# First block's scan of states read from PSUM, and the steps beside both attentions dealt anew

## The chip, the cores and the metric

The kernel runs on one core of a Trainium2 chip. The time is the device time of one execution in microseconds (us). The engines named below are PE (TensorE, the matrix engine; PEld is its weight load), DVE (VectorE), ACT (ScalarE), POOL (GpSimd) and SP (SyncE, which issues the transfers). All data is float32. SBUF is the on-chip memory that every engine reads; PSUM is the memory that PE writes, here two tensors `acc` and `wrk` of four banks each, 128 partitions by 512 numbers a bank.

## The reference, cut to what matters

Two transformer blocks of two layers each run one after the other on 256 tokens of width 1024. Of a layer of the first block only the mixer matters here:

```python
mod = silu(c) @ w_ada[l] + b_ada[l]      # 6 x 1024: shifts, scales, gates; layer 0 needs them first
a_out = dsa_mixer(aq, ak, av, ...)       # 6 heads of attention, 256 tokens, top-64 mask
b_out = hgrn2_mixer(bq, bf, bi, bg, ...) # 6 heads of a gated recurrence
#   state = exp(b_last) * state + k^T v  # one 64 x 64 state a head, a decay for each row
x = x + g1 * (concat(a_out, b_out, c_out) @ w_out[l])
```

A layer of the second block has three kinds of heads, the projections that feed them, and a retention:

```python
o_nsa = nsa_mixer(...)          # 6 heads, 3 branches each: compressed, selected, window
o_mla = mla_mixer(...)          # 5 heads; q and k come from latents cq, ckv by small matmuls
o_ret = retention_mixer(...)    # 5 heads, needs rq, rk, rv, rg
x = x + concat(o_nsa, o_mla, o_ret) @ w_out[l]
```

## The kernel before, in words

The order of the instructions on each engine is written out by hand. Each engine runs its own list, and waits on counters (`pe_done`, `act_done`, `dve_done`, `pool_done`) that the others raise; nothing is reordered.

**An attention** (`att_pe`, `att_act`, `att_dve`) runs over units, a unit being one branch of one head. Units go in pairs. For a unit PE computes the scores (L1023, into `wrk` banks 0 and 1), DVE masks them and takes the maximum (L1085, L1089), ACT takes the exponential (L1138), DVE divides (L1102, L1106), PE turns the result (L1036), ACT copies it back to SBUF (L1153), and PE multiplies by the values (L1056, L1058). DVE then copies the head's sum from `acc` (L1130). This chain has waits in it, and a function `beside(u)` lays other work into it, at unit `u`, on each engine.

**The first block.** Six units. The recurrence works in 16 blocks of 16 tokens: a loop of 16 bands on PE and DVE (L1380, L1496 to L1522) computes what happens inside a block, and its last piece is named "band end". Then the keys are turned (L1389). For each of three pairs of heads, `kv_pe` (L1405) makes the key-value products of all 16 blocks into `acc` banks 2 and 3 (8 matmuls of 256 columns on quarter tiles of the array, 64 by 64, called a set below), `kv_act` (L1417) copies them to SBUF in another order, `states_dve` (L1555) runs the recurrence over the blocks with two scans in place, and `inter_pe` (L1434) multiplies by the queries. PE makes the sets beside units 0, 1, 2 and the `inter` products beside units 3, 4, 5; the scans stand beside units 2, 3, 4. A set may start only when ACT has copied the one before it.

In layer 0 four column groups of `w_ada` (6 to 9) stand between band end and the attention, as steps "a" and "s": "a" is 8 matmuls of 512 columns (L672), which ACT copies (L680), "s" is 4 matmuls of one column that sum the copy (L687), and DVE adds the bias (L695, `mods`). In the tables "a 6" and "s 6" are the two for group 6.

**The second block.** 23 units: 18 of the first kind of heads (12 with full scores, then 6 with 15 columns) and 5 of the second kind (units 18 to 22). The table `BESIDE` gives for each unit the steps beside it: "p" is a projection (8 matmuls, L877, L880 or L893, copied by ACT), "r" a rotary turn (one matmul L922 and three DVE instructions L931 to L936), "m" a small product of a latent (L3027, copied by ACT at L3048). The steps alternate between `acc` banks 2 and 3, so the PE part of step n waits until step n-2 has been read. Units 18 to 22 need all "m" steps and the rotary turns of the "mq" ones.

Of the kernel before, what the change touches and what calls it, by code (L numbers as in the profile page):

```python
# [9 lines left out]
ALU = mybir.AluOpType  # L10
# [4 lines left out]
S = 256  # L15
# [3 lines left out]
HD = 64  # L19
# [147 lines left out]
def stream_items():  # L167
# [27 lines left out]
    for layer in range(DEPTH):  # L195
        after += [("in2", layer, i) for i in range(3)] + [("cmp", layer)] + [("in2", layer, i) for i in range(3, 6)]
        after += [("mla", layer), ("in2", layer, 6), ("decay", layer)] + [("out2", layer, h) for h in range(2)]
# [41 lines left out]
def program(nc, given, out, known, stop=None, dumps=None):  # L239
# [3 lines left out]
    with ExitStack() as ctx:  # L243
# [765 lines left out]
        def head_sum(b):  # L1009

            return acc[b["p0"]:b["p0"] + HD, b["head"] % 2, b["col"]:b["col"] + S]
# [238 lines left out]
        def branches1(l):  # L1250
            out = []
            for h in range(6):
                p0, j = HD * (h % 2), h // 2
                out.append(dict(q=s_q[p0:p0 + HD, j, :], k=s_k[p0:p0 + HD, 0, :], v=lambda t: s_v[:, t, :], mask=s_mask, head=h,
                                kind="causal", scale=float(HD) ** -0.5, gate=None, opens=True, last=True, p0=p0, col=0,
# [93 lines left out]
        r_pick = [Z(o, 4, HD) for o in (5888, 6144, 6400, 4352, 10640, 10896, 11152, 1536, 12176, 12432, 12688, 12944)]  # L1349
# [42 lines left out]
        def kv_pe(pe, l, a):  # L1392
# [17 lines left out]
        def kv_act(act, l, a):  # L1410
            if a == 2:
                act.wait_ge(dve_done, at("dve", "c out", l, 1))

            act.wait_ge(pe_done, at("pe", "kv", l, a))
            by_half = r_state[a].rearrange("p v (t r b) -> p r t b v", t=2, r=2)
# [117 lines left out]
        def picks_pool(pool, l, a):  # L1533
# [6 lines left out]
            else:  # L1540
                pool.wait_ge(dve_done, at("dve", "band end", l) if l else at("dve", "mods", 0, 9))
# [6 lines left out]
        def states_dve(dve, l, a):  # L1548

            dve.wait_ge(act_done, at("act", "kv", l, a))  # L1550
            dve.wait_ge(pool_done, at("pool", "wide", l, a))
            wide = r_wide[a].rearrange("p v b -> p (v b)")
            for i in range(HD // SCAN):
                part = r_state[a][:, SCAN * i:SCAN * (i + 1), :].rearrange("p v b -> p (v b)")
                dve.tensor_tensor_scan(part, wide, part, 0.0, ALU.mult, ALU.add)\  # L1555
                   .then_inc(dve_done, up("dve", "states", l, a) if i == HD // SCAN - 1 else up("dve"))
# [257 lines left out]
        def act_from(wait_names):  # L1814
# [6 lines left out]
        BESIDE_BANDS[0].update({8: ("a 4", "a 5"), 9: ("s 4", "s 5"), 10: ("p bg1",), 12: ("p bg2",),  # L1821
                                15: ("a 6", "a 7", "s 6", "a 8", "s 7", "a 9", "s 8", "s 9")})
        BESIDE_BANDS[1].update({8: ("p bg1",), 10: ("p bg2",)})
# [1891 lines left out]
```

## Time and profile before

| | us |
|---|---|
| median of 3 runs | 2350.98 |
| lowest, highest run | 2350.53, 2360.26 |
| the profiled execution's own time | 2354.34 |
| its span, first to last instruction | 2352.2 |

| stage of the profiled execution | from, us | to, us |
|---|---|---|
| first block, layer 0: last band matmul to output projection | 150.67 | 194.21 |
| first block, layer 1: scores of the attention to output projection | 586.38 | 616.55 |
| second block, layer 0: from the turned unit 11 to the retention | 1651.40 | 1707.80 |
| second block, layer 1: the same | 2041.15 | 2097.80 |

In a row of the timeline the first two numbers are the start and the length. A bracket at its end gives how long the engine stood idle just before, and what released it. A matmul in float32 leaves two records, so "x16" is 8 matmuls. A row whose instructions had a gap between them is longer by the gap. PEclk is the clock that PE was granted, 1.00 being 2.4 GHz and 0.50 being 1.2 GHz.

### The profile page before, as it was taken

To read this page: it belongs to the slowest core of one execution; us is meant where nothing else is said; L and a number is where in the kernel's file an instruction comes from. 1 tells how busy PE (TensorE), PEld (TensorE's weight loads), DVE (VectorE), ACT (ScalarE), POOL (GpSimd) and SP (SyncE) were. 2 spreads that over 40 slices of the span, in tenths; PEclk is the share of its full clock that TensorE was granted. 3 is DMA by queue.
4 is the path that set the end of the run, shared out by engine and by line. 5 is a ranking of instruction groups with operands and counts; after the bars stand their busy time and mean duration, and the time that the engine had idled before them with its cause. 6 is when DMAs were issued, how large, how long until landed. Compare 5 with 4: busy or idle time off the path is not lost.

```text
span 2352.2 us, 36220 instructions
## 1 busy us (share of the span) xinstructions
PE 2264.7 (96%) x15501; PEld 1596.1 (68%) x15502; DVE 920.6 (39%) x2174; ACT 381.8 (16%) x893; POOL 27.6 (1%) x52
## 2 busy tenths in 40 slices
PE   7989999999999999998999999989999999999999
PEld 5868998877763434433444444357679998769999
DVE  3663887548420000000000000034657734547764
ACT  3231100022320000000000000025421002531100
POOL 1010000001000000000000000000000000000000
PEclk8997999999899999999999999999999999999999
DMA  9571478944069999999988999992325463423441
GB/s 349 187 251 37 157 255 299 378 143 143 14 240 374 373 412 410 408 411 409 407 299 355 409 410 409 413 325 92 107 72 179 164 188 117 159 74 108 167 157 54
DMA packets 242163, 582.98 MB, mean 248 GB/s; under 512 B 24250, under 2 KB 108738, under 8 KB 229716
## 3 DMA queue, kind: packets, MB, share of 16 engines
q1 hardware_dynamic: 241428, 580.52, 66.6%
q8 instruction: 125, 2.05, 0.4%
q14 instruction: 34, 0.28, 0.0%
q0 software_dynamic: 576, 0.13, 0.0%
HBM read 579.58 MB, written 1.05 MB: 247 GB/s over the span
## 4 chain that ended last, share of the span: by engine, by line
PE 87%; DMA 6%; DVE 4%; ACT 1%; SPq 1%; issue 1%; DVEq 0%; ACTq 0%
PE wrk L2496 13%; PE acc L877 9%; PE acc L3335 5%; PE acc L3303 5%; PE acc L2556 5%; PE wrk L2481 4%; PE wrk L3335 4%; PE wrk L3303 4%; DMA ring<-in_moe_w_gate_dram 3%; PE acc L880 3%; PE acc L1660 3%; PE wrk L2503 3%; PE acc L1680 3%; PE wrk L1660 3%; PE acc L954 2%; PE acc L2539 2%
## 5 line engine op out<-in xcount | busy, mean ns | idle before, releaser
L2496 PE MATMUL wrk<-ring,hT 128*64 128x512 f32 (+1 forms) x1792 | 348.7, 542 | 11.8 <-DMA ring<-in_moe_w_up_dram 5.8
L2740 DVE TENSOR_TENSOR scratch<-scratch,wrk 128x512 f32<-128x512 f32 (+4 forms) x32 | 24.5, 767 | 793.2 <-PE wrk L2496 584.5
L2496 PEld LDWEIGHTS wrk<-ring,hT 128*64 128x64 f32 x1792 | 125.7, 137 | 211.7 <-issue 186.3
L877 PE MATMUL acc<-hT,ring 128*128 128x256 f32 x1024 | 231.7, 381 | 3.7 <-DVE scratch L936 2.9
L877 PEld LDWEIGHTS acc<-hT,ring 128*128 128x128 f32 x1024 | 191.4, 190 | 33.7 <-DVE scratch L936 3.9
L2556 PE MATMUL acc<-ring,scratch 128*64 128x512 f32 x784 | 177.2, 597 | 8.5 <-DMA ring<-in_moe_w_down_dram 7.7
L3380 DVE TENSOR_TENSOR ring<-ring 128x512 f32<-128x512 f32 (+1 forms) x192 | 155.2, 863 | 1.2
L2556 PEld LDWEIGHTS acc<-ring,scratch 128*64 128x64 f32 x784 | 53.8, 136 | 113.1 <-issue 101.8
L3335 PE MATMUL acc<-scratch,ring 128*128 128x128 f32 x1024 | 117.6, 275 | 0.0
L3335 PEld LDWEIGHTS acc<-scratch,ring 128*128 128x128 f32 x1024 | 116.0, 192 | 0.0
L2675 ACT ACTIVATE scratch<-wrk 128x512 f32<-128x512 f32 (+4 forms) x32 | 21.1, 661 | 483.6 <-PE wrk L2528 483.6
L2481 PE MATMUL wrk<-ring,hT 128*128 128x512 f32 x224 | 96.9, 593 | 0.5 <-DMA ring<-in_moe_w_gate_dram 0.5
L3335 PE MATMUL wrk<-scratch,ring 128*128 128x128 f32 x768 | 89.0, 275 | 0.0
L3303 PE MATMUL acc<-mixT,ring 128*128 128x128 f32 x768 | 88.4, 275 | 0.0
L3335 PEld LDWEIGHTS wrk<-scratch,ring 128*128 128x128 f32 x768 | 87.4, 192 | 0.0
L3303 PEld LDWEIGHTS acc<-mixT,ring 128*128 128x128 f32 x768 | 87.0, 192 | 0.0
L880 PE MATMUL acc<-ring,hT 128*128 128x384 f32 (+5 forms) x384 | 81.3, 368 | 4.7 <-ACT scratch L910 2.9
L1680 PE MATMUL acc<-scratch,ring 128*128 128x256 f32 x352 | 77.2, 380 | 4.4 <-DMA ring<-in_ffn_w_down_dram 4.4
L910 ACT ACTIVATE scratch<-acc 128x256 f32<-128x256 f32 (+6 forms) x118 | 41.3, 361 | 231.9 <-PE acc L877 158.2
L2481 PEld LDWEIGHTS wrk<-ring,hT 128*128 128x128 f32 x224 | 42.3, 190 | 53.1 <-issue 53.1
L2503 PE MATMUL wrk<-ring,hT 128*32 128x256 f32 (+1 forms) x1536 | 77.6, 354 | 0.0
L880 PEld LDWEIGHTS acc<-ring,hT 128*128 128x128 f32 x384 | 60.7, 195 | 23.8 <-ACT scratch L910 4.3
(464 smaller groups left out, 3001.1 us busy)
## 6 DMA issues: line engine op xcount, KB each, us to landing
ring<-in_moe_w_gate_dram SPq DMA_DIRECT2D x56, 2048.0 KB, 19.1
ring<-in_moe_w_up_dram SPq DMA_DIRECT2D x56, 2048.0 KB, 21.1
ring<-in_moe_w_down_dram SPq DMA_DIRECT2D x56, 2048.0 KB, 22.6
ring<-in_w_ada_dram SPq DMA_DIRECT2D x24, 2048.0 KB, 17.0
ring<-in_w_up_dram SPq DMA_DIRECT2D x32, 1024.0 KB, 6.8
ring<-in_w_down_dram SPq DMA_DIRECT2D x32, 1024.0 KB, 6.4
ring<-in_w_out_dram SPq DMA_DIRECT2D x8, 2048.0 KB, 8.6
ring<-in_w_in_dram SPq DMA_DIRECT2D x10, 1536.0 KB, 9.6
```

What stands on the lines that cost most here:

```text
L877: mm = pe.matmul(acc[p0:p0 + m, bank, 0:S], cols(k), hT[:, k, :], start=(k == 0), stop=(k == KD - 1))
L880: mm = pe.matmul(acc[:, bank, 0:m], hT[:, k, t], cols(k), start=(k == 0), stop=(k == KD - 1))
L954: pe.matmul(accv[:, 4 * h + m, :], w[:, k, m * P:(m + 1) * P], mixT[:, k, :], start=(k == ks[0] and m % 2 == 0), stop=False, skip_group_ch ...
L1660: mm = pe.matmul(PRODUCT[x][:, t * P:(t + 1) * P], stationary[x][:, k, t * P:(t + 1) * P], moving[x][:, k, :], start=(k == 0), stop=(k == ...
L1680: mm = pe.matmul(accv[:, m, :], w[:, j, m * P:(m + 1) * P], DENSE_TILES[:, 4 * g + j, :], start=(g == 0 and j == 0 and m % 2 == 0), stop=( ...
L2481: mm = pe.matmul(flat_wrk[:, lo + c * 512:lo + (c + 1) * 512], hT[:, k, 0:P], w[:, at_, c * 512:(c + 1) * 512], start=(k == 0), stop=(k == ...
L2496: mm = pe.matmul(flat_wrk[h * HD:h * HD + HD, lo:lo + n2], hT[:, k, 0:HD], w[:, at_, h * n2:(h + 1) * n2], start=(k == 0), stop=(k == KD - ...
L2503: mm = pe.matmul(flat_wrk[quarter(c), lo + n2:lo + n2 + n4], hT[:, k, LIGHT:MIDDLE], w[:, at_, c * n4:(c + 1) * n4], start=(k == 0 and n2 ...
L2556: mm = pe.matmul(acc[h * HD:h * HD + HD, 0, :], turned[:, at_:at_ + HD], w[:, j, h * 512:(h + 1) * 512], start=(g == 0 and n == 0), stop=( ...
L3303: mm = pe.matmul(up_region(x)[:, t * P:(t + 1) * P], stationary[x][:, k, t * P:(t + 1) * P], moving[x][:, k, :], start=(k == 0), stop=(k = ...
L3335: mm = pe.matmul(PRODUCT[x][:, m * P:(m + 1) * P], stationary[x][:, t, m, :], moving[x][:, t, :], start=(i == 0 and t == 0 and m == 0), st ...
L3380: ins = dve.tensor_tensor(part(out_), part(a), part(b), ALU.subtract)
```

## The change

Four things change.

**The scan reads PSUM.** `kv_pe` now makes the products in the order in which the scan reads them: 16 matmuls of 128 columns (32 values by 4 blocks), each written with a stride of 16 numbers in its bank, in two turns, the second of which waits until the first has ended (PE waits on its own counter). The moving operand is read with its two inner dimensions swapped. `kv_act` is gone. `states_dve` scans straight from `acc` banks 2 and 3 into SBUF, beside units 0, 1 and 2 instead of 2, 3 and 4. A set waits for the two scans of the one before; the first `inter` waits for the scans of the third set.

**The a and s steps of layer 0** leave the place ahead of the attention and stand beside its units (`BESIDE_UNITS`), all in `acc` bank 0. Both heads of a pair now use bank 1. "a 7" waits until DVE has read "s 6", and so on.

**The second block's steps** from unit 12 on are dealt anew: the "m" steps go forward and stand in groups of three, the projections rv0, rv1, rg1, rg2 go back to units 18 to 21, and one rotary turn stands beside each unit. The loads of `w_in_2` part 5 and of the latents' weights swap places.

**Small ones.** Four of POOL's buffers (`r_pick` 8 to 11) move, since their old place is now in use, and with it goes POOL's wait for the s steps; `gain_dve(0, 1)` stands behind the attention.

```diff
         def kv_pe(pe, l, a):
...
-                pe.wait_ge(act_done, at("act", "kv", l, a - 1))
+                pe.wait_ge(dve_done, at("dve", "states", l, a - 1, 1))
             pe.wait_ge(pool_done, at("pool", "pick", l, 4 * a + 3))
-            for t in range(2):
-                for turn in range(2):
-                    for h in range(2):
-                        r = HD * ((h + turn) % 2)
-                        mm = pe.matmul(acc[HD * h:HD * h + HD, 2 + r // HD, S * t:S * t + S], r_kT[r:r + HD, 2 * a + t, HD * h:HD * h + HD],
-                                       r_pick[4 * a + 2 * h + t][r:r + HD].rearrange("p b v -> p (b v)"), start=True, stop=True,
-                                       skip_group_check=True)
-            mm.then_inc(pe_done, up("pe", "kv", l, a))
-
-        def kv_act(act, l, a):
...
-            for r in range(2):
-                act.activation(by_half[:, r], acc[:, 2 + r, :].rearrange("p (t b v) -> p t b v", t=2, v=HD), ACT.Copy)\
-                   .then_inc(act_done, up("act", "kv", l, a) if r else up("act"))
+            for turn in range(2):
+                if turn:
+                    pe.wait_ge(pe_done, at("pe", "kv half", l, a))
+                for t in range(2):
+                    for r in range(2):
+                        i = (r + turn) % 2
+                        own = acc[:, 2 + i, :].rearrange("p (v t r b) -> p t r v b", t=2, r=2, b=4)
+                        rows = slice(HD * r, HD * r + HD)
+                        for h in range(2):
+                            mm = pe.matmul(own[HD * h:HD * h + HD, t, r], r_kT[rows, 2 * a + t, HD * h:HD * h + HD],
+                                           r_pick[4 * a + 2 * h + t][rows, :, SCAN * i:SCAN * (i + 1)].rearrange("p b v -> p v b"),
+                                           start=True, stop=True, skip_group_check=True)
+                mm.then_inc(pe_done, up("pe", "kv" if turn else "kv half", l, a))
...
         def inter_pe(pe, l, a):
-            pe.wait_ge(dve_done, at("dve", "states", l, a))
+            pe.wait_ge(dve_done, at("dve", "states", l, a, 1))
             if a == 0:
-                pe.wait_ge(act_done, at("act", "kv", l, 2))
+                pe.wait_ge(dve_done, at("dve", "states", l, 2, 1))
...
         def states_dve(dve, l, a):
 
-            dve.wait_ge(act_done, at("act", "kv", l, a))
             dve.wait_ge(pool_done, at("pool", "wide", l, a))
+            dve.wait_ge(pe_done, at("pe", "kv", l, a))
...
-                dve.tensor_tensor_scan(part, wide, part, 0.0, ALU.mult, ALU.add)\
+                dve.tensor_tensor_scan(part, wide, acc[:, 2 + i, :], 0.0, ALU.mult, ALU.add)\
...
+        BESIDE_UNITS = ((("a 6",), ("s 6", "a 7"), ("s 7", "a 8"), ("s 8", "a 9"), ("s 9",), ()), ((),) * 6)
+        MODULATED = sum(BESIDE_UNITS[0], ())
...
+        def step1_bank(l, n):
+
+            return 0 if steps1(l)[n] in MODULATED else bank1(n)
...
+            def beside(u):
+                if u < 3:
+                    states_dve(dve, l, u)
+                for step in BESIDE_UNITS[l][u]:
+                    step1_dve(dve, l, step)
+                if u == 5:
+                    head_sum_dve(dve, l)
...
-                  ("p rq2", "r kpe"), ("p rk1", "r rq0"), ("p rk2", "m mq0"), ("p rk0", "m mq1", "r mq0"),
+                  ("p rq2", "r kpe"), ("p rk1", "r rq0"), ("m mq0", "m mq1", "m mk0", "r rq1"), ("p rk2", "r mq0"),
```

On PE, in layer 0 of the first block, these rows stood one after the other (L672 an a step, L687 an s step, L1389 the turned keys, L1405 a set, L1023 scores, L1036 a turned unit):

```order
L672 MATMUL acc<-ring,vec_rows 32x512 x16
L687 MATMUL acc<-const,scratch 128x1 x4
L672 MATMUL acc<-ring,vec_rows 32x512 x8
L687 MATMUL acc<-const,scratch 128x1 x4
L672 MATMUL acc<-ring,vec_rows 32x512 x8
L687 MATMUL acc<-const,scratch 128x1 x8
L1389 MATMUL acc<-const,mixT 128x128 x6
```

and in the changed kernel, from the turned keys on (L1410 is the new set):

```order
L1410 MATMUL acc<-scratch 64x32x4 x16
L687 MATMUL acc<-const,scratch 128x1 x4
L672 MATMUL acc<-ring,vec_rows 32x512 x8
L1036 MATMUL wrk<-const,scratch 128x128 x3
L1410 MATMUL acc<-scratch 64x32x4 x16
L687 MATMUL acc<-const,scratch 128x1 x4
L672 MATMUL acc<-ring,vec_rows 32x512 x8
```

The keys and the scores now come first, and each a step stands behind a set and an s step, ahead of the next turned unit.

On DVE the changed kernel has at the same place, behind the masks and the division of a unit, the two scans and the bias of the s step (L695), ahead of the next unit's mask:

```order
L1106 TENSOR_SCALAR scratch<-scratch,stat 128x128
L1106 TENSOR_SCALAR scratch<-scratch,stat 128x256
L1548 SCALAR_TENSOR_TENSOR hT<-scratch,acc 128x512 x2
L695 TENSOR_TENSOR mods<-acc,vec 128x4
L1085 ISA scratch,stat<-wrk,scratch 128x128
```

So "a 7", which waits for L695, waits for both scans too.

On PE in the second block, at units 12 to 14, the difference is this (L3027 before and L3031 after are the m steps, L893 and L877 projections, L922 a rotary turn, L1033 a turned unit, L1023 scores):

```order
-L893 MATMUL acc<-hT,ring 64x256 x16
-L3027 MATMUL acc<-scratch,ring 96x256 x2
+L877 MATMUL acc<-hT,ring 128x256 x8
 L922 MATMUL acc<-scratch,const 96x256
 L1033 MATMUL wrk<-const,scratch 15x128 x2
-L3027 MATMUL acc<-scratch,ring 96x256 x2
-L3027 MATMUL acc<-scratch,ring 64x256
+L3031 MATMUL acc<-scratch,ring 96x256 x2
+L3031 MATMUL acc<-scratch,ring 64x256 x2
```

A projection is followed by one rotary turn, and the m steps have moved together.

## Rows read from the trace of the kernel before

**Rows 1.** The page: PE's share of the span, and the chain by engine.
```profile
PE 2264.7 (96%) x15501; PEld 1596.1 (68%) x15502; DVE 920.6 (39%) x2174; ACT 381.8 (16%) x893; POOL 27.6 (1%) x52
...
PE 87%; DMA 6%; DVE 4%; ACT 1%; SPq 1%; issue 1%; DVEq 0%; ACTq 0%
```

**Rows 2.** Timeline of PE, first block, layer 0.
```profile
151.22 3.64 PE L672 MATMUL acc<-ring,vec_rows 128*32 128x512 f32 x32
154.79 1.05 PE L687 MATMUL acc<-const,scratch 128*128 128x1 f32 x8
...
162.27 0.85 PE L1389 MATMUL acc<-const,mixT 128*128 128x128 f32 x6
...
164.03 1.09 PE L1405 MATMUL acc<-scratch 64*64 64x256 f32 x16
165.94 0.93 PE L1023 MATMUL wrk<-scratch 64*128 64x128 f32 x8 [0.82 <-DVE stat L1089]
...
169.00 1.09 PE L1405 MATMUL acc<-scratch 64*64 64x256 f32 x16 [1.33 <-ACT hT L1417]
...
172.12 1.99 PE L1405 MATMUL acc<-scratch 64*64 64x256 f32 x16 [1.55 <-ACT hT L1417]
...
194.21 3.78 PE L954 MATMUL acc<-mixT,ring 128*128 128x256 f32 x8
...
208.81 4.58 PE L954 MATMUL acc<-mixT,ring 128*128 128x256 f32 x20
```

**Rows 3.** Timelines of DVE and ACT, same place: band end, scans, copy.
```profile
153.07 0.69 DVE L1522 TENSOR_TENSOR mixT<-mixT,scratch 128x48 f32<-128x48 f32 x1
...
170.83 2.33 DVE L1555 TENSOR_TENSOR_SCAN hT<-scratch,hT 128x512 f32<-128x512 f32 x2
...
167.06 1.89 ACT L1417 ACTIVATE hT<-acc 128x512 f32<-128x512 f32 x2
```

**Rows 4.** Stretches at half clock: window, length, busy by engine, PEclk, DMA, GB/s.
```profile
171.50:178.20 6.70, 6.08 (x41) 3.27 (x41) 4.01 (x13) 3.80 (x9) 0.00 (x0) 0.50 0.00 0
182.00:204.80 22.80, 21.99 (x173) 18.24 (x174) 7.05 (x15) 4.54 (x10) 0.00 (x0) 0.50 0.00 1
616.55:618.30 1.75, 1.75 (x6) 1.48 (x5) 1.54 (x3) 0.30 (x1) 0.00 (x0) 0.50 0.00 0
1707.40:1714.30 6.90, 6.50 (x28) 4.67 (x30) 2.35 (x6) 0.44 (x1) 0.00 (x0) 0.51 0.00 0
```

**Rows 5.** Timeline of PE, first block, layer 1: sets and first inter.
```profile
593.25 1.78 PE L1405 MATMUL acc<-scratch 64*64 64x256 f32 x16 [0.23 <-ACT hT L1417]
...
597.08 1.09 PE L1405 MATMUL acc<-scratch 64*64 64x256 f32 x16 [1.56 <-ACT hT L1417]
...
600.36 3.48 PE L1434 MATMUL acc<-scratch,hT 64*64 64x16 f32 x60
```

**Rows 6.** Groups by line and form, 160 to 195 us: quarter-tile weight loads.
```profile
L1434 PEld LDWEIGHTS acc<-scratch 64*64 64x64 f32 x60 | 3.4, 199 | 0.3 <-DVE mixT L1130 0.3
...
L1405 PEld LDWEIGHTS acc<-scratch 64*64 64x64 f32 x48 | 1.8, 160 | 4.4 <-ACT hT L1417 3.4 <-ACT scratch L1468 0.4 <-issue 0.4
```

**Rows 7.** Timeline of PE, second block, layer 1.
```profile
2041.15 3.62 PE L877 MATMUL acc<-hT,ring 128*128 128x256 f32 x16
...
2075.53 3.72 PE L877 MATMUL acc<-hT,ring 128*128 128x256 f32 x16 [0.32 <-DVE scratch L936]
...
2085.29 3.72 PE L877 MATMUL acc<-hT,ring 128*128 128x256 f32 x16 [1.13 <-DVE scratch L936]
...
2096.12 0.65 PE L1056 MATMUL acc<-scratch 128*64 128x256 f32 x2 [1.43 <-DVE mixT L1130]
...
2097.80 1.23 PE L3117 MATMUL wrk<-scratch 64*128 64x256 f32 x4 [0.60 <-DVE mixT L1130]
```

**Rows 8.** Timelines of DVE and ACT, same stage: latents, rotary turn, exponential.
```profile
2041.27 0.48 DVE L2960 SCALAR_TENSOR_TENSOR scratch<-scratch,vec 128x256 f32<-128x256 f32 x1
...
2042.77 0.42 DVE L936 TENSOR_TENSOR scratch<-scratch 64x256 f32<-64x256 f32 x1
...
2043.73 0.31 ACT L1138 ACTIVATE scratch<-scratch,stat 128x15 f32<-128x15 f32 x1 [0.87 <-DVE stat L1089]
```

More of the change, by code:

```diff
@@ L195, in stream_items @@
     for layer in range(DEPTH):
-        after += [("in2", layer, i) for i in range(3)] + [("cmp", layer)] + [("in2", layer, i) for i in range(3, 6)]
-        after += [("mla", layer), ("in2", layer, 6), ("decay", layer)] + [("out2", layer, h) for h in range(2)]
+        after += [("in2", layer, i) for i in range(3)] + [("cmp", layer)] + [("in2", layer, i) for i in range(3, 5)]
+        after += [("mla", layer), ("in2", layer, 5), ("in2", layer, 6), ("decay", layer)] + [("out2", layer, h) for h in range(2)]
         n = D_FF // 512
@@ L1009, in head_sum @@
         def head_sum(b):
-            return acc[b["p0"]:b["p0"] + HD, b["head"] % 2, b["col"]:b["col"] + S]
+            return acc[b["p0"]:b["p0"] + HD, b["bank"], b["col"]:b["col"] + S]
         def att_scores_pe(pe, tag, pair, branches):
@@ L1254, in branches1 @@
                 out.append(dict(q=s_q[p0:p0 + HD, j, :], k=s_k[p0:p0 + HD, 0, :], v=lambda t: s_v[:, t, :], mask=s_mask, head=h,
-                                kind="causal", scale=float(HD) ** -0.5, gate=None, opens=True, last=True, p0=p0, col=0,
+                                kind="causal", scale=float(HD) ** -0.5, gate=None, opens=True, last=True, p0=p0, bank=1, col=0,
                                 over=[h - 2] if h >= 2 else [], place=mixT[p0:p0 + HD, j, :],
@@ L1348, in program @@
         r_kT, r_squares = Z(7568, 6, P), Z(1536, 3, S)
-        r_pick = [Z(o, 4, HD) for o in (5888, 6144, 6400, 4352, 10640, 10896, 11152, 1536, 12176, 12432, 12688, 12944)]
+        r_pick = [Z(o, 4, HD) for o in (5888, 6144, 6400, 4352, 10640, 10896, 11152, 1536, 1792, 2048, 7184, 4608)]
         r_root = stat[:, 112:124]
@@ L1539, in picks_pool @@
                 pool.wait_ge(dve_done, at("dve", "band end", l))
-            else:
-                pool.wait_ge(dve_done, at("dve", "band end", l) if l else at("dve", "mods", 0, 9))
             for n in range(4 * a, 4 * a + 4):
@@ L1833, in steps1 @@
                 steps += BESIDE_BANDS[l].get(j, ())
-            return steps
+            return steps + sum(BESIDE_UNITS[l], ())
         def number1(l, name):
@@ L1841, in bank1 @@
             return n % 4 if n < FIRST_BESIDE else 2 + n % 2
+        def step1_bank(l, n):
+            return 0 if steps1(l)[n] in MODULATED else bank1(n)
         def bank1_read(l, n, bank):
-            users = [i for i in range(n) if bank1(i) == bank]
+            users = [i for i in range(n) if step1_bank(l, i) == bank]
             return step1_read(l, users[-1]) if users else None
@@ L1870, in step1_pe @@
             kind, _, name = step.partition(" ")
-            bank, bank_read = bank1(n), bank1_read(l, n, bank1(n))
+            bank, bank_read = step1_bank(l, n), bank1_read(l, n, step1_bank(l, n))
+            if step == MODULATED[0]:
+                bank_read = (act_done, at("act", "kT", l))
             if kind == "p":
@@ L1945, in beside @@
                     inter_pe(pe, l, u - 3)
+                for step in BESIDE_UNITS[l][u]:
+                    step1_pe(pe, l, step)
             att_pe(pe, tag, branches1(l), beside)
@@ L1990, in beside @@
             def beside(u):
-                if u < 3:
-                    kv_act(act, l, u)
+                for step in BESIDE_UNITS[l][u]:
+                    step1_act(act, l, step)
             att_act(act, tag, branches1(l), beside)
@@ L2036, in block1_dve @@
                     topk_mask_dve(dve, l)
+            def beside(u):
+                if u < 3:
+                    states_dve(dve, l, u)
+                for step in BESIDE_UNITS[l][u]:
+                    step1_dve(dve, l, step)
+                if u == 5:
+                    head_sum_dve(dve, l)
+            att_dve(dve, tag, branches1(l), beside)
             if l == 0:
                 gain_dve(dve, 0, 1)
-            def beside(u):
-                if 2 <= u < 5:
-                    states_dve(dve, l, u - 2)
-                elif u == 5:
-                    head_sum_dve(dve, l)
-            att_dve(dve, tag, branches1(l), beside)
             head_norm_dve(dve, l)
@@ L3078, in branches2 @@
                                 scale=float(HD) ** -0.5, gate=lambda t, c=3 * h + br: n_gate[:, t, c:c + 1], opens=br == 1 and i < 2,
-                                last=br == 0, head=2 * i + g_, p0=HD * (h % 2), col=S * (i // 2), over=[],
+                                last=br == 0, head=2 * i + g_, p0=HD * (h % 2), bank=g_, col=S * (i // 2), over=[],
                                 place=mixT[HD * (h % 2):HD * (h % 2) + HD, h // 2, :],
@@ L3088, in branches2 @@
                                 mask=K("causal"), kind="causal", scale=96.0 ** -0.5, gate=None, opens=True, last=True, p0=p0, head=6 + h,
-                                col=0, over=((0, 4), (1, 5), (6,), (7,), (8,))[h],
+                                bank=h % 2, col=0, over=((0, 4), (1, 5), (6,), (7,), (8,))[h],
                                 place=mixT[p0:p0 + HD, 3 + h // 2, :], mask_ready=[],
```

13 lines of the change are left out of this document (4 added, 9 removed), and 6 rows, old and new, of the table BESIDE.

## The prediction

> **What bounds the kernel now.** I read the page first: PE is busy for 96% of the span, and 87% of the chain that ended last runs through it [rows 1]. So only what PE does, or waits for, can move the time, and the evictions on ACT that the change removes are worth just the PE idle time they cause. Next I read the timeline of PE around the places that the diff touches, four stages of 30 to 60 us each. In the first block, layer 0, PE runs from 151.22 to 194.21, and from 151.22 to 162.27 it works through the a and s steps without a gap [rows 2]. The idle time comes behind: 1.33 and 1.55 us before the second and third set, both for ACT's copy, and 0.82 us before scores [rows 2]. The reader is to see that the a and s steps are not waits that can be filled but 11 us of PE work that only moves. In layer 1 the same two waits are 0.23 and 1.56 us [rows 5]. In the second block the idle time stands late, where two rotary turns share a unit: 0.32 and 1.13 us, and 1.43 and 0.60 us in the tail [rows 7]. Last I read the windows for the granted clock: PE runs at 1.2 GHz from 171.5 to 178.2 and from 182.0 to 204.8, in the tail of the second block for 6.9 us, but for only 1.75 us of layer 1's output projection [rows 4]. It fell after stretches with waits in them, and it rose after dense ones.
>
> All waits that the change can remove add up to some 12 us over the four stages, about 0.5% of the time, and about 0.5% is also what a measurement of this kernel can tell from no change.
>
> **One set.** Before, 8 matmuls of 256 columns take 1.09 us at full clock [rows 2]. Now there are 16 of 128 columns with the same number of columns in all, and PE waits once for its own first half. No row shows this form. The lower bound is 1.0 us, since the columns are the same (a gain of 0.1 has no mechanism here but is not excluded). The upper bound is what the columns take if the four quarter tiles don't overlap: the output projection takes 4.58 us for 20 records of 256 columns [rows 2], 0.23 us a record, so 0.23 us for two records of 128, and 16 times that is 3.7 us. The nearest row is `inter`, the other stream of quarter tiles: 30 matmuls in 3.48 us [rows 5], 0.116 us each, bound by how fast they follow each other. 16 of them take 1.9 us, and I take 2.0 with the wait in the middle. That is 0.9 us more a set at full clock; at half clock a set took 1.78 [rows 5] to 1.99 us already [rows 2], and there I add 0.2 us.
>
> The order of access is in doubt too. `inter` loads weights with a stride between its numbers and a load takes 199 ns; the load of a set, whose numbers lie side by side, takes 160 ns, although half of those ran at half clock [rows 6]. So a stride costs something on the read side. The Trainium skill, "SBUF — State Buffer" (section "Door 1: The DMA port swizzle"), says it in general: "any non-contiguous PSUM access pattern significantly slows down matmuls", and a read from SBUF is slowed once each access goes to another line of 16 bytes. By that rule a set nears 3.7 us and the sum is +9.7; by the row the stride costs a quarter of a load and the sum is the one below.
>
> **One scan pair** takes 2.33 us from SBUF [rows 3], 1.17 us for 512 numbers. Reading PSUM could cost more or nothing; DVE's masks and head copies read PSUM all along, and I keep 2.33, with 2.0 and 4.7 as ends (a small gain, or twice the time).
>
> **First block, layer 0.** Against 151.22 to 194.21:
> - three sets, 0.9 us each: +2.7;
> - the waits for ACT's copy go: 1.33 + 1.55 = -2.9; the 0.82 us before the scores is now covered by "a 6": -0.8;
> - the third set and the work to 178.2 ran at half clock. The set alone lost 1.99 - 1.09 = 0.9, and of 6.08 us busy [rows 4] at most half, 3.0, was lost. With four a steps in it this stretch should stay at full clock: -2.7;
> - at the start the scores need band end, 153.07 + 0.69 = 153.76 [rows 3], and the turned keys alone, 0.85 us, end at 152.1. The a steps used to cover this: +1.7;
> - "a 7" waits until DVE has added the bias of "s 6", and that stands behind the two scans, which wait for the set. From the end of the set DVE needs 2.33 and some 0.3 for the bias and hand-overs; PE has only the s step, 1.05 us [rows 2]. So PE idles 1.6 us, and again before "a 8"; before "a 9" the scans are done and about 0.3 is left: +3.5. Behind the waiting a step stands the turned unit on PE, for which ACT and the value matmuls wait.
> Sum: 2.7 - 2.9 - 0.8 - 2.7 + 1.7 + 3.5 = +1.5 us.
>
> The output projection behind it starts at 194.21 and stays at half clock until 204.8, 10.6 us, a loss of 5.3. In layer 1 the same stage is at half clock for 1.75 us, a loss of 0.9 [rows 4]. Where in this stage the clock rises is not set by the change, so I take the mean of the two, 3.1: -2.2 us.
>
> DMA and POOL are no term: the picks of the third set are ready before it, and the ring slots that the a steps free later hold weights of the next stage, some 40 us away.
>
> **First block, layer 1.** No a steps cover anything. Two sets at half clock and one at full: 0.2 + 0.2 + 0.9 = 1.3. A set waits for 2.33 of scans instead of 1.89 of copies [rows 3], +0.4 twice, less a part covered: +0.7. The first `inter`, which began at 600.36 without a wait [rows 5], now waits for the third set's scans: +0.4. Sum +2.4 us.
>
> **Second block,** for each layer. Spreading the rotary turns takes away 0.32 and 1.13, and with projections beside the last units half of the 1.43 goes: -2.1. The m steps come one projection earlier, and stop there: "m mq0" would start at 2041.15 [rows 7] but the latents are ready at 2041.75, and "m mq1" needs the bank of the rotary turn that ends at 2043.2 [rows 8]: +0.6 and +0.5. The third of the group waits for ACT, whose exponentials start at 2043.73 ahead of the copies [rows 8]; this and the other groups I set at +0.5, against 0.6 of smaller waits that go. Sum -1.1, in two layers -2.2 us.
>
> **Sum.** +1.5 - 2.2 + 2.4 - 2.2 = -0.5 us. The profiled execution took 2354.3 (span 2352.2 and 2.1 around it), so it would take 2353.8; it was 3.4 us above the median, which is in the scatter of the three runs. From the median 2351.0 I forecast 2350.5.
>
> **Rivals.**
> - *Strides* (slower). If the quarter tiles stop overlapping, a set takes 3.7 us, 1.7 above my value, six times: +10.2, so 2360.7. For it: the strided weight loads. Against it: 4 numbers still lie side by side in PSUM, and the strided loads of `inter` cost 39 ns, not a multiple. It decides the sign from about 2.1 us a set. A scan pair of 4.7 us would do as much, 2.4 at the five waits for scans, with nothing in the trace for it. Chance 0.15 together.
> - *Cheap sets* (faster). A set stays at 1.1 us: 0.9 off in each of four sets at full clock and 0.2 in two: 2346.5. Chance 0.17.
> - *Clock* (faster). Denser work keeps PE at 2.4 GHz: the rest of the output projection's loss (3.1), some 2.1 between 182 and 194, where `inter` does not scale with the clock, and half of 6.5 us busy in both tails (6.4): -12.1, so 2338.9. Against it: `inter` runs of 3.5 us stand in the same place, and the clock fell behind them before. In full 0.05, half of it (2344.7) 0.13.
> - *Waits win* (slower). The scans' waits let the clock fall in layer 0 as before (+2.7) and the groups of m steps eat the second block's gain (+2.2): 2355.4. Chance 0.2.
> - The forecast itself: 0.3, with 2348 to 2353 as its own range.
>
> Only the ends of the strides and the clock rivals reach 11.8 us, 0.5%. Faster 0.06, same 0.89, slower 0.05. The range 2342 to 2359 leaves out the full clock rival and the far end of strides.
>
> **What would show it.** Right: L1410 about 2.0 us a set; in layer 0 two idle stretches of about 1.6 us on PE before L672, released by DVE L695; in layer 1 the first L1429 some 2.4 us later after the first scores; in the second block no wait above 1 us before a projection from unit 17 on, and a new wait before L3031 at unit 12. The forecast is wrong if the sets are off by over 0.5 us, if the clock differs from before by more than 5 us of half clock in all, or if a stage that the diff does not touch changes its length.

## The result and the profile after

| | before | changed |
|---|---|---|
| median, us (12 runs each, side by side) | 2352.9 | 2362.45 |
| lowest, highest | 2348.32, 2360.42 | 2358.04, 2366.21 |
| profiled execution, its span | 2354.34, 2352.2 | 2358.04, 2356.1 |

The ratio is 1.0034, with a 95% interval from 1.0023 to 1.0044: by it the change makes the kernel about 8 us slower (the medians lie 9.5 us apart). All ratios here are of the fast executions; one of 5892 us and one of 2397 us, in the two kernels with moved code below, are left out. The forecast was 2350.5, within 2342 to 2359, and the measured median lies above that range. The profiled execution of the changed kernel was the fastest of its twelve, so the profiles differ by only 3.7 us. The stages below are therefore read in several profiles each.

The page of the changed kernel answers to [rows 1]: PE has 96 more matmul records (48 matmuls) and 96 more weight loads, and its share of the chain falls from 87 to 86%.

```profile
PE 2263.3 (96%) x15597; PEld 1594.1 (68%) x15598; DVE 920.9 (39%) x2174; ACT 371.4 (16%) x881; POOL 27.6 (1%) x52
...
PE 86%; DMA 6%; DVE 5%; issue 1%; SPq 1%; ACT 1%; DVEq 0%; ACTq 0%
```

The timeline of PE in layer 0 of the first block, changed kernel, answers to [rows 2]. L1410 is the new set.

```profile
149.57 0.62 PE L1380 MATMUL wrk<-scratch,const 128*128 128x24 f32 x4 [1.09 <-DVE scratch L1499]
...
152.81 1.40 PE L1023 MATMUL wrk<-scratch 64*128 64x128 f32 x8 [1.91 <-DVE mixT L1517]
154.14 2.58 PE L1410 MATMUL acc<-scratch 64*64 64x128 f32 x32
...
159.83 2.45 PE L1410 MATMUL acc<-scratch 64*64 64x128 f32 x32
...
164.96 1.92 PE L672 MATMUL acc<-ring,vec_rows 128*32 128x512 f32 x16 [1.70 <-DVE mods L695]
...
167.29 2.42 PE L1410 MATMUL acc<-scratch 64*64 64x128 f32 x32
...
172.38 2.50 PE L672 MATMUL acc<-ring,vec_rows 128*32 128x512 f32 x16 [1.69 <-DVE mods L695]
...
183.58 3.64 PE L672 MATMUL acc<-ring,vec_rows 128*32 128x512 f32 x16 [0.35 <-DVE mods L695]
...
201.76 3.24 PE L954 MATMUL acc<-mixT,ring 128*128 128x256 f32 x8
```

The waits are where the prediction put them: 1.91 us for band end, then 1.70, 1.69 and 0.35 us for the bias. The sets at full clock take 2.42 to 2.45 us instead of 1.09. "a 8" and "a 9" take 2.50 and 3.64 us where "a 7" takes 1.92: the clock is down again. On DVE the reason for the 1.70 us is plain, the scans (L1548) stand ahead of the bias, and they take the same 2.33 us from PSUM as from SBUF [rows 3]:

```profile
162.43 2.33 DVE L1548 TENSOR_TENSOR_SCAN hT<-scratch,acc 128x512 f32<-128x512 f32 x2 [1.27 <-PE acc L1410]
164.68 0.14 DVE L695 TENSOR_TENSOR mods<-acc,vec 128x4 f32<-128x4 f32 x1
```

Layer 1 of the first block (with [rows 5]) has its waits before the second and third set and, new, a short one before the first `inter` (L1429):

```profile
598.98 2.53 PE L1410 MATMUL acc<-scratch 64*64 64x128 f32 x32 [1.21 <-DVE hT L1548]
...
604.02 2.50 PE L1410 MATMUL acc<-scratch 64*64 64x128 f32 x32 [1.68 <-DVE hT L1548]
...
609.13 3.48 PE L1429 MATMUL acc<-scratch,hT 64*64 64x16 f32 x60 [0.18 <-DVE scratch L1548]
```

Then a place that the diff doesn't touch, the norm behind the experts of the first block (L837). PE stops in it for 2.43 us, released by nothing that the profile shows:

```profile
1565.98 0.51 PE L837 MATMUL wrk<-scratch,const 128*128 128x256 f32 x1
1568.92 0.48 PE L837 MATMUL wrk<-scratch,const 128*128 128x256 f32 x1 [2.43 <-issue]
```

In the kernel before this norm has no gap. And the tail of the second block, with [rows 7] and the last of [rows 4]: the retention's matmuls take 0.71 us instead of 1.23, at full clock, and 5.24 us pass from the first of them to the output projection, instead of 7.76.

```profile
2102.91 0.65 PE L1056 MATMUL acc<-scratch 128*64 128x256 f32 x2 [0.58 <-ACT scratch L1153]
...
2104.37 0.71 PE L3121 MATMUL wrk<-scratch 64*128 64x256 f32 x4 [0.60 <-DVE mixT L1130]
...
2109.61 4.58 PE L954 MATMUL acc<-mixT,ring 128*128 128x256 f32 x20
```

### The profile page after: what moved, and what is told of

It reads as the page before. It is cut to its first block, busy times and chain, and to the rows that moved or that the text cites. A ratio compares the mean times of both kernels' runs of the same rounds, so it can differ in the third digit from the quotient of the medians.

```text
span 2356.1 us, 36398 instructions
## 1 busy us (share of the span) xinstructions
PE 2263.3 (96%) x15597; PEld 1594.1 (68%) x15598; DVE 920.9 (39%) x2174; ACT 371.4 (16%) x881; POOL 27.6 (1%) x52
## 4 chain that ended last, share of the span: by engine, by line
PE 86%; DMA 6%; DVE 5%; issue 1%; SPq 1%; ACT 1%; DVEq 0%; ACTq 0%
PE wrk L2500 13%; PE acc L877 8%; PE acc L3339 5%; PE acc L3307 5%; PE acc L2560 5%; PE wrk L2485 4%; PE wrk L3339 4%; PE wrk L3307 4%; DMA ring<-in_moe_w_gate_dram 4%; PE acc L880 3%; PE wrk L2507 3%; PE acc L1653 3%; PE acc L1673 3%; PE wrk L1653 3%; PE acc L954 2%; PE acc L2543 2%
## 5 line engine op out<-in xcount | busy, mean ns | idle before, releaser
L877 PE MATMUL acc<-hT,ring 128*128 128x256 f32 x1024 | 231.4, 380 | 0.8 <-DVE hT L852 0.4
L877 PEld LDWEIGHTS acc<-hT,ring 128*128 128x128 f32 x1024 | 191.4, 190 | 29.8 <-issue 3.5
```

The costliest lines, as they stand in the source:

```text
L877: mm = pe.matmul(acc[p0:p0 + m, bank, 0:S], cols(k), hT[:, k, :], start=(k == 0), stop=(k == KD - 1))
```

## Parts alone

Four kernels take the change apart. "Scan" is the PSUM scan with its sets, "dealing" the a and s steps beside the units of layer 0, "table" the second block's steps and stream order.

The table alone (kernel before, with these lines of the change and the rest of the table, which the front shows in part):

```diff
-                  ("p rq2", "r kpe"), ("p rk1", "r rq0"), ("p rk2", "m mq0"), ("p rk0", "m mq1", "r mq0"),
+                  ("p rq2", "r kpe"), ("p rk1", "r rq0"), ("m mq0", "m mq1", "m mk0", "r rq1"), ("p rk2", "r mq0"),
```

> The kernel before with one part of the change: the second block's steps dealt anew (its table of steps and the stream's order). Theory A (the parts add up as the two profiles show them, the clock included): the two attentions of the second block are 0.5 and 0.9 us shorter in work and 2.6 and 2.5 us shorter in their retention tails, which run at the full clock; 6.5 us less in all, ratio 0.9972. Theory B (the tails' clock was the chance of one execution, only the work is shorter): 1.4 us less, ratio 0.9994, and the tail from the last projection's matmuls to the first output projection matmul of 20 keeps about 7.8 us in this profile. Between them: 3 to 4 us less if one tail in two runs at the full clock.

Measured: 0.9962 (0.9948 to 0.9975), 9 us faster. Theory A. Both tails run at full clock, as two windows of this kernel show, one over the whole attention of layer 0 and one over the last 64 us of layer 1's (window, length, PE busy and its records, PEclk, DMA, GB/s):

```profile
1591.88:1713.19 121.31, 115.97 (x734) 0.99 0.30 100
2036.00:2099.65 63.65, 58.48 (x324) 1.00 0.26 86
```

This is no chance. In all nine profiles of kernels with the new table both tails take 5.23 or 5.24 us; in the five with the old one they take 7.1 to 8.6. From the first waiting scores of the second block to layer 1's output projection the nine take 506.2 to 507.9 us and the five 512.8 to 518.5.

The first block alone (scan and dealing, old table; the edits from here on are against the changed kernel, and cut):

```diff
-                  ("p rq2", "r kpe"), ("p rk1", "r rq0"), ("m mq0", "m mq1", "m mk0", "r rq1"), ("p rk2", "r mq0"),
+                  ("p rq2", "r kpe"), ("p rk1", "r rq0"), ("p rk2", "m mq0"), ("p rk0", "m mq1", "r mq0"),
```

> The change without its second part: the first block changed (scan out of PSUM, adaptive steps dealt to the attention's units), the second block as before. Theory A: 9.5 us measured for the whole change plus the 6.5 us that the second block gives back, 16 us more, ratio 1.0068. Theory B: 9.5 plus 1.4, 11 us more, ratio 1.0046. The profile is to show the stretch from the end of the last band to the output projection of layer 0 at about 51 us against 43.0, and layer 1's at about 33.6 against 30.2 in either case.

Measured: 1.0073 (1.0059 to 1.0087), 17 us slower, theory A. With the table's -9 that makes the +8 of the whole: the two parts add.

The scan alone (with the old table too):

```diff
+                                15: ("a 6", "a 7", "s 6", "a 8", "s 7", "a 9", "s 8", "s 9")})
...
-        BESIDE_UNITS = ((("a 6",), ("s 6", "a 7"), ("s 7", "a 8"), ("s 8", "a 9"), ("s 9",), ()), ((),) * 6)
+        BESIDE_UNITS = (((),) * 6, ((),) * 6)
```

> The kernel before with the PSUM scan alone: products laid in the scan's order in two halves, no eviction, scans one unit apart; the adaptive steps stay behind the last band. Theory A (the dearer sets decide): each of the six sets is about 2.5 us instead of 1.1 to 2.0, and the units wait 1.2 to 1.7 us for the scan of the set before in layer 1; 3.4 us more in each layer, 7 us in all, ratio 1.0029. Theory C (the dealing of the adaptive steps is what costs, the scan is paid by the eviction it saves): 0 to 2 us more, ratio under 1.001.

Measured: 1.0039 (1.0025 to 1.0053), 9 us slower. That is theory A, whose 1.0029 lies within the interval, but not layer by layer: layer 0 is only 2.0 us longer and layer 1 4.3, where it has 3.4 for each. The rest is the stretch with the stop in the norm, 2.33 us here too, which the theory doesn't have.

The dealing alone (old table, and the old sets, copies and scans):

```diff
+                if u < 3:
+                    kv_act(act, l, u)
...
-                if u < 3:
-                    states_dve(dve, l, u)
+                if 2 <= u < 5:
+                    states_dve(dve, l, u - 2)
```

> The kernel before with the adaptive steps a 6 to s 9 dealt to the attention's units alone; key-value sets, evictions on ScalarE and scans as before. Theory A (waits of a 7 and a 8 came from VectorE's scans standing ahead of the reads in units 1 and 2; here the scans start at unit 2): the wait of a 7 goes, a 8 and a 9 keep one each, layer 0 gains the start of the attention but loses up to 5 us of clock in it; 0 to 3 us more, ratio 1.000 to 1.0013. Theory C (the dealing costs by itself, because TensorE runs thinner behind the last band and drops its clock): 6 us more or over, ratio 1.0026 or more, and the half clock covers more than 20 us of this stretch.

Measured: 1.0016 (1.0006 to 1.0025), 3.7 us slower, between the theories; layer 0 is 1.7 us longer, and no wait before an a step exceeds 0.35 us.

The stages, each from the timelines of the profiles (us):

| | layer 0: last band matmul to output projection | layer 1: scores to output projection | norm behind the experts to second block |
|---|---|---|---|
| before; table alone; before, code moved (below) | 43.5, 43.5, 43.5 | 30.2, 30.2, 30.1 | 36.0, 36.0, 41.0 |
| scan alone | 45.5 | 34.4 | 40.0 |
| dealing alone | 45.2 | 33.2 | 37.3 |
| changed; first block alone; changed, code moved | 52.2, 53.5, 53.0 | 33.6, 33.6, 33.7 | 40.1, 39.9, 37.2 |

So in layer 0 scan and dealing cost 2.0 and 1.7 us apart and 9.4 together. Only together do a set, two scans and an s step with its bias chase one another within one unit.

The table shows one thing more. With the dealing alone layer 1 is 3.0 us longer too, though its sets, copies and scans there are the old ones; of its edits only the bank of the heads' sums and the place of POOL's buffers, with its wait, reach that layer. Windows over the stage, first the kernel before, then the dealing alone:

```profile
586.38:616.55 30.17, 26.95 (x295) 0.67 0.01 4
```

```profile
582.34:615.56 33.22, 29.32 (x294) 0.55 0.01 4
```

Idle time grew by 0.7 us only (the wait before the second set is 1.33 instead of 0.23 us, the one before the third 1.19 instead of 1.56); the other 2.4 us are the same matmuls at a lower granted clock, 0.55 against 0.67. So 2 to 3 us of this stage can be clock alone, and what a kernel costs in it is not the price of its sets.

## The stop in a place that was not touched

All seven profiles of kernels with the long sets whose code is otherwise in its place show the stop (2.2 to 2.8 us), the three with the short ones don't. The sets added 192 instructions to PE's list, ahead of a jump: the experts' work is written twice, for few and for many tokens, and PE jumps over the second, which never runs here, straight to the norm. Two kernels move only what lies in that second part.

```diff
                 if k % 2:
                     mm.then_inc(last_share, 1)
+            for _ in range(126):
+                pe.wait_ge(last_weights, 1)
```

> The changed kernel with 64 more instructions in TensorE's code for the many-token case of the experts, which is jumped over in every run: nothing more is executed, only the code that the jump lands on moves by 64 places. The six longer sets added 192 instructions ahead of that jump, 192 plus 64 is 256. Theory F (the 2.2 to 2.4 us without a releaser in the norm behind the experts, seen in all three kernels with the long sets and in none without, is code that has not arrived behind the jump; it also keeps TensorE at half clock): the stall goes, the stretch from the first L837 to the first waiting L1023 of block two is 36 us again instead of 40.1, and the kernel is 4 us faster than the changed one: ratio to before 1.0017 instead of 1.0034. Theory N (the stall comes of the different times at which work arrives, not of where the code lies): no change, 1.0034.

> The kernel before with 192 instructions in the same code that is never run, so that the jump lands where it lands in the changed kernel. Theory F: a stall of 2.3 us in L837 after its seventh matmul and 4 us more in all, ratio 1.0017. Theory N: the same time as before, 1.0000, no stall.

The second has 382 waits in the same loop. Two waits make one instruction, so the loops make 63 and 191 instructions, one fewer than the expectations say. Measured: the changed kernel with the first loop 1.0021 (1.0006 to 1.0035), no stop, 37.2 us for the stretch instead of 40.1; the kernel before with the second 1.0016 (1.0004 to 1.0029), and 41.0 us instead of 36.0, with this in its timeline:

```profile
1556.54 0.63 PE L837 MATMUL wrk<-scratch,const 128*128 128x256 f32 x1
1559.99 0.80 PE L837 MATMUL wrk<-scratch,const 128*128 128x256 f32 x1 [2.83 <-issue]
```

It is the same matmul at which the changed kernel stops. So the place of the code decides it, as theory F has it: nothing more ran, and the kernel before got the stall and the changed one lost it. The two mended kernels below, with the first loop, are without the stop as well. In times the second is shown by its interval; the first agrees with -3 us but its interval touches the changed kernel's. The Trainium skill, "Runtime: NRT & Kernel Launch" (section "Instruction fetch mechanics"), says that instructions come in blocks of 256 and that a jump out of the window of two blocks forces a fetch. 192 + 63 = 255 fits but for one place: this move gave back nearly the old alignment. That a fetch is what PE waits for, and that the next block, just behind the landing place, is what comes late, is my reading of it; no run shows a fetch.

## What a set costs

> The changed kernel with its sets read and written in contiguous order (128 columns in a row out, four pieces of 32 in), so the scan's states are in another order than they should be; nothing else differs, and all sizes and counts stay. Theory L (a set is bound by its 32 matmuls with their weight loads and the wait for its own half, not by strides): a set still takes 2.3 to 2.6 us. Theory S (strides cost): a set falls to 1.7 us or less, half the columns' time and the wait of 0.55.

```diff
-                        own = acc[:, 2 + i, :].rearrange("p (v t r b) -> p t r v b", t=2, r=2, b=4)
+                        own = acc[:, 2 + i, :].rearrange("p (t r b v) -> p t r b v", t=2, r=2, b=4)
...
-                                           r_pick[4 * a + 2 * h + t][rows, :, SCAN * i:SCAN * (i + 1)].rearrange("p b v -> p v b"),
+                                           r_pick[4 * a + 2 * h + t][rows, :, SCAN * i:SCAN * (i + 1)],
```

Measured: 1.42 us a set at full clock, theory S; 2357.96 in its one run. Which side, reads or writes? One kernel makes only the writes contiguous, the other only the reads:

```diff
-                        own = acc[:, 2 + i, :].rearrange("p (v t r b) -> p t r v b", t=2, r=2, b=4)
+                        own = acc[:, 2 + i, :].rearrange("p (t r v b) -> p t r v b", t=2, r=2, b=4)
```

> The changed kernel with only the writes of its sets made contiguous (128 numbers in a row of PSUM in place of runs of four, 64 bytes apart); the pieces land in another order than the scans take them, so the states are of the wrong order. The reads stay strided (each number 256 bytes from the one before). With both made contiguous a set fell from 2.45 to 1.42 us. Theory R (the strided read of the moving operand costs it): a set at full clock stays at 2.4 us. Theory P (the strided write into PSUM costs it): it falls to 1.4 us. Both in part: about 1.9.

```diff
-                                           r_pick[4 * a + 2 * h + t][rows, :, SCAN * i:SCAN * (i + 1)].rearrange("p b v -> p v b"),
+                                           r_pick[4 * a + 2 * h + t][rows, SCAN * i:SCAN * (i + 1), :],
...
-                pool.tensor_tensor(r_pick[n], K("blocks4").unsqueeze(2).broadcast_to([P, 4, HD]),
-                                   b_i[:, t, (2 * a + h) * HD:(2 * a + h + 1) * HD].unsqueeze(1).broadcast_to([P, 4, HD]),
+                pool.tensor_tensor(r_pick[n], K("blocks4").unsqueeze(1).broadcast_to([P, HD, 4]),
+                                   b_i[:, t, (2 * a + h) * HD:(2 * a + h + 1) * HD].unsqueeze(2).broadcast_to([P, HD, 4]),
```

> The changed kernel, its result unchanged, with GpSimd laying down the masked products in the order in which the sets read them (value index outside, block inside), so that each matmul reads 128 numbers in a row; the writes into PSUM stay strided. Theory R: a set at full clock is 1.4 us, layer 0 loses 3 to 4 us of its 9.3, the waits of layer 1 for the scans take the place there; 3 to 4 us faster than the changed kernel, ratio to before 1.0018 to 1.0022. Theory P: sets stay at 2.4 us, ratio 1.0034. A danger for both: GpSimd's products may take longer in this order and come too late.

With contiguous writes alone, in one run of 2364.54 us, a set at full clock is as slow as ever:

```profile
162.38 2.44 PE L1410 MATMUL acc<-scratch 64*64 64x128 f32 x32
```

With contiguous reads, writes strided:

```profile
160.36 1.42 PE L1410 MATMUL acc<-scratch 64*64 64x128 f32 x32 [0.30 <-DVE hT L1548]
...
168.23 1.42 PE L1410 MATMUL acc<-scratch 64*64 64x128 f32 x32
...
594.61 2.35 PE L1410 MATMUL acc<-scratch 64*64 64x128 f32 x32 [1.66 <-DVE hT L1548]
```

The strided read costs 1.0 us a set, the strided write nothing. At half clock the set takes 2.35 us against 2.50 to 2.76, so the read costs only 0.2 to 0.4 there. Time: 1.0019 (1.0006 to 1.0031), 3.5 us less than the changed kernel. The two intervals overlap, so it is layer 0 that shows the gain, 49.3 us against 52.2 to 53.5. In layer 1 nothing came of it, 34.4 us against 33.6: its sets ran almost wholly at half clock (PEclk of the stage is 0.60 against 0.65), and the waits before the second and third grew from 2.9 to 3.35 us. POOL's products took 669 instead of 648 ns. What is left above the old 1.09 us is 0.3. The wait in the middle of a set, for which the weight loads idle 2.6 us over six sets, 0.4 each, would cover it; no run takes that wait away.

## Waits of the dealt steps, and mended versions

```diff
             def beside(u):
+                for step in BESIDE_UNITS[l][u]:
+                    step1_dve(dve, l, step)
                 if u < 3:
                     states_dve(dve, l, u)
-                for step in BESIDE_UNITS[l][u]:
-                    step1_dve(dve, l, step)
```

> The changed kernel with VectorE's order in the first three units turned: the read of the adaptive sums (L695) goes ahead of the scans. Theory A (the dealt steps wait because their bank's reader stands behind two scans): the waits of 1.70 and 1.69 us before L672 in units 1 and 2 shrink to under 0.7, and with less idle time less half clock: 3 to 6 us faster than the changed kernel, ratio to before 1.0008 to 1.0021. Theory W (the wait moves: now a scan waits for TensorE's sum and the next set waits for the scan): the waits before L1410 grow by as much, ratio 1.0034 as the changed kernel.

Measured: 1.0021 (1.0009 to 1.0033), 3 us less than the changed kernel. The intervals overlap here too, but both waits before L672 are 0.35 us, and layer 0 takes 48.6 us instead of 52.2 to 53.5, as theory A says; in layer 1 a set still waits 1.6 and 2.0 us for the scans.

```profile
165.82 3.55 PE L672 MATMUL acc<-ring,vec_rows 128*32 128x512 f32 x16 [0.35 <-DVE mods L695]
...
173.53 1.92 PE L672 MATMUL acc<-ring,vec_rows 128*32 128x512 f32 x16 [0.35 <-DVE mods L695]
```

The last two join the repairs: the scan alone with the new table, contiguous reads and moved code; and the whole change with all three. Of the first, beside the reads shown above:

```diff
-        BESIDE_UNITS = ((("a 6",), ("s 6", "a 7"), ("s 7", "a 8"), ("s 8", "a 9"), ("s 9",), ()), ((),) * 6)
+        BESIDE_UNITS = (((),) * 6, ((),) * 6)
...
+            for _ in range(126):
+                pe.wait_ge(last_weights, 1)
```

> The second block as changed, the PSUM scan with contiguous reads of its products, the adaptive steps left behind the last band, and the code behind the jump moved to where it lay before. By the terms measured so far, against the kernel before: layer 0 of the first block +2.0 less up to 3 for three cheaper sets, layer 1 +3.5 less up to 2, the code stall 0, the second block -8.5: -8 us in all, ratio 0.9966 (0.9953 to 0.998). It beats the second block's change alone (0.9962) only if the evictions that went on ScalarE had cost something that is not yet seen (rival: under 0.995).

> The changed kernel with all three repairs: contiguous reads in the sets, VectorE's reads of the adaptive sums ahead of the scans, code behind the jump moved by 64. By the single terms, if they add: 8.0 (changed kernel) less 4.3 (sums first), 3.9 (sets) and 4 (stall) is -4 us, ratio 0.9983. Rival (the repairs overlap, since all of them thin out the same waits and half-clock time): 0 us, ratio 1.000.

Measured: 0.9982 (0.9971 to 0.9992) and 0.9989 (0.9979 to 0.9998). Both beat the kernel before; neither beats the table alone, 0.9962. The second came out as its single terms add up. The first missed its expectation by 4 us: as the sets got cheaper the waits for the scans grew, in layer 0 to 1.69 and 2.00 us from 1.39 and 1.71, and layers 0 and 1 take 44.9 and 34.6 us, hardly other than the 45.5 and 34.4 of the scan alone.

```profile
168.59 1.42 PE L1410 MATMUL acc<-scratch 64*64 64x128 f32 x32 [1.69 <-DVE hT L1548]
...
172.54 2.35 PE L1410 MATMUL acc<-scratch 64*64 64x128 f32 x32 [2.00 <-DVE hT L1548]
```

So with the scans in PSUM the pace is theirs: both banks are taken until DVE has scanned, behind its own masks, while the old ACT copy freed them in 1.89 us and let the scans follow later. The best version measured is the kernel before with the second block's table alone.

## Why the prediction was wrong, step by step

| step | predicted | in the profiles (means of the rows named) |
|---|---|---|
| first block, layer 0 | +1.5 | +9.4 (52.9 of three against 43.5 of three) |
| output projection and on to layer 1 | -2.2 | -1.3 (389.7 of three against 391.1 of three, which lie from 388.8 to 392.3) |
| first block, layer 1 | +2.4 | +3.5 (33.6 against 30.2) |
| norm behind the experts | not seen | +4.0 (40.0 against 36.0) |
| second block | -2.2 | -9.2 (506.9 of the nine with the new table against 516.1 of the five with the old) |
| sum | -0.5 | +6.4; timed +8 (5.4 to 10.4) |

**Layer 0.** The step that failed is "With four a steps in it this stretch should stay at full clock: -2.7". Idle time came out as put, +1.5 predicted (-2.9 - 0.8 + 1.7 + 3.5) and +1.8 measured. The sets, which the sum has at +2.7 against three of 1.09 us, take 7.45 us, +4.2. PE is busy 6.85 us longer in all, so the term of the clock, put at -2.7, came out at +2.7, and at +3.4 and +3.7 in two other profiles: the other matmuls are the same as before and took longer. Windows of the kernel before, then of the changed one, from the last band matmul to the output projection:

```profile
150.67:194.21 43.54, 38.73 (x401) 0.78 0.46 153
```

```profile
149.57:201.76 52.19, 45.58 (x449) 0.76 0.39 128
```

Half clock is 0.22 x 2 x 43.5 = 19 us before and 0.24 x 2 x 52.2 = 25 us after (0.73 and 29 us in the two other profiles). The a steps were dense work while they stood together; dealt out between waits they ran at 1.2 GHz themselves ("a 9" 3.64 us, "a 7" 1.92). I counted the waits as lost time only, and their effect on the clock of what stands around them as a gain. That the waits are the cause is what the rows agree with, and not shown by itself: with the bias ahead of the scans idle time is 2.7 us shorter and half clock covers 21 us of the stage, but dealing alone, with less idle time than the kernel before (3.7 against 4.8 us), has 21 us of it too against 19.

**The sets.** The value of 2.0 us was too low by 0.45: the stride on the read side costs 1.0 us, which I had weighed at a quarter of a weight load and the Trainium skill at more. I had misread the row, too: of the set's loads a third, not half, ran at half clock, and over the two sets at full clock a load takes 132 ns, in the kernel before:

```profile
L1405 PEld LDWEIGHTS acc<-scratch 64*64 64x64 f32 x32 | 1.0, 132 | 2.3 <-ACT hT L1417 1.6 <-ACT scratch L1468 0.4
```

Against the 199 ns of `inter` [rows 6] that is half a load more at full clock and not a quarter, so the row spoke louder for the *strides* rival than the prediction has it. (At half clock the set's loads take 214 ns, and there the stride shows nothing.) The rule of the Trainium skill has two halves, "SBUF — State Buffer", section "Door 1: The DMA port swizzle": the one on reads that each touch another 16-byte line agrees (2.45 against 1.42 us); the one that "any non-contiguous PSUM access pattern significantly slows down matmuls" does not show here (2.44 with contiguous, 2.45 with strided writes). The Trainium skill gives no size there; the 3.7 us that I hung on it was my own upper bound. So the rival *strides* had the right sign and too high a price, and that its 2360.7 lies near the measured 2362.45 is luck: the stop in the norm and the clock made up what the sets did not cost. The scan pair at 2.33 us was right.

**Output projection.** The size was close, but the kernel before itself, with its code moved, shows 388.8 us here. It is a chance of the execution, not an effect of the change.

**Layer 1.** The waits were right: 1.21 and 1.68 us before the sets and 0.18 before `inter` make +1.3 us where +1.1 was put. Three sets cost 2.8 us more (7.61 against 4.85) instead of 1.3. But the clock of this stage moves by as much from kernel to kernel, as the dealing alone shows, so the close total of +3.5 is no proof of the terms.

**Second block.** The waits above 1 us are gone from unit 17 on and the new ones before L3031 (0.4 to 0.7 us) came as foretold. The failure is that the tails were left at half clock: I gave their 6.4 us to the *clock* rival, at 0.05 in full. The table alone gives 9 us. This gain is the reason why the whole came out at +8 and not at the first block's +17.

**The untouched norm** was named as a sign that the forecast is wrong, and it was one; the 192 new instructions stood in the diff, but I had counted their execution only. The sign of the clock came as well: over the whole span PEclk was 0.976 before and 0.980 in the changed kernel's profile, some 19 us less at half clock, where more than 5 either way was to be a sign.

## What to carry to other kernels

Price a wait in a sparse stage with the clock of the work around it: where dense work was dealt out into waits it ran slower here, and with the long waits gone from a tail the whole tail ran at full speed. Before giving a stage's change to one term, compare the granted clock in the stage. Moving the reader of a shared buffer from an idle engine to a busy one cost more here than the copy it saved, since the buffer came free later. When one stage that the edit doesn't touch grows, look for a stop without a releaser, and test it by moving code that never runs.

## What the runs showed of the hardware

- Strided reads of a matmul's moving operand (float32, 256 bytes apart) took a set of 32 quarter-tile records from 1.42 to 2.45 us at 2.4 GHz, and from 2.35 to between 2.50 and 2.76 at 1.2. Writes to PSUM in runs of four numbers, 64 bytes apart, took nothing.
- A jump over 63 or 191 more instructions that never run moved a stop of 2.2 to 2.8 us out or in; with the half clock around it the whole was 3 to 5 us.
- In the kernel before, weight loads of a quarter tile took 132 ns with the numbers side by side and 199 with a stride, at 2.4 GHz; at 1.2 GHz they took 214 and 199.
- A scan reads PSUM as fast as SBUF, 2.33 us for two of 512 numbers.
- The stretch through the experts took from 906.1 to 910.5 us from profile to profile, with no relation to the edits. The changed kernel's profiled execution had 906.1, which may be one reason why it was faster than its other runs; what sets it was not found.
